# Low halves written over the raw weight tile, four tiles of high halves, and a raw slot that is reloaded after TensorE's use

## The reference, cut to what matters

```python
for l in range(2):
    xn = rmsnorm(x, norm1_g)
    u  = xn @ w_in                                   # 1024 x 9216
    ya, yb, yc, yd = mixers(u)                       # conv, pooling, RG-LRU, conformer conv
    m  = sum_k sigmoid(u_gate_k + b_k) * (y_k @ w_p_k)
    x  = x + m @ w_out
    xn = rmsnorm(x, norm2_g)
    q  = xn @ peer_wq;  s = q . keys                 # top-16 per head, softmax gates
    x  = x + sum over chosen experts of gate * gelu(xn . u_tab[e]) * v_tab[e]
y = rmsnorm(x, final_g)
```

## Time and profile before

| | us |
|---|---|
| three runs: median (lowest to highest) | 2685.22 (2684.17 to 2688.6) |
| profiled execution, its own time | 2685.49 |
| its span, first to last instruction | 2683.4 |
| TensorE matmuls, busy | 2602.2 |
| Pool, busy | 1981.5 |
| DVE, busy | 1512.3 |
| ACT, busy | 1444.6 |

### The profile page before, as it was taken

One profiled execution on the slowest core, in us unless ns is written; L12 is line 12 of the kernel. 1 busy time (PEld: TensorE's weight loads), 2 busy tenths in 40 slices (PEclk: granted clock), 3 DMA queues, 4 the chain that ended last, 5 costly groups with the idle time before them and its releaser, 6 DMA issues. The chain is left out here.

```text
span 2683.4 us, 58960 instructions
## 1 busy us (share of the span) xinstructions
PE 2602.2 (97%) x19532; PEld 2584.3 (96%) x19532; DVE 1512.3 (56%) x3456; ACT 1444.6 (54%) x2996; POOL 1981.5 (74%) x1528
## 2 busy tenths in 40 slices
PE   6999989999999999999989999999999999999997
PEld 6999989999999999999989998899999999999997
DVE  6588232995578733333375863249936786333333
ACT  4764544444666544444447645444456665444444
POOL 6788666888655688888777876668875557888885
PEclk9999999999999999999999999999999999999999
DMA  5555654555433455555454556444553334555554
GB/s 173 152 154 161 157 164 137 169 164 165 133 117 110 135 164 164 181 165 164 150 155 151 159 155 170 158 141 157 169 164 120 113 116 143 163 164 181 165 164 137
DMA packets 126362, 410.67 MB, mean 153 GB/s; under 512 B 20160, under 2 KB 24640, under 8 KB 125504
## 3 DMA queue, kind: packets, MB, share of 16 engines
q1 hardware_dynamic: 120304, 403.37, 48.7%
q10 hardware_dynamic: 5968, 6.22, 1.0%
HBM read 403.32 MB, written 6.22 MB: 153 GB/s over the span
## 5 line engine op out<-in xcount | busy, mean ns | idle before, releaser
L586 POOL TENSOR_TENSOR w_low<-raw,w_high 128x512 fp32r<-128x512 f32 x1498 | 1964.5, 1318 | 660.6 <-ACT w_high L872 463.5
L872 ACT ACTIVATE w_high<-raw 128x512 fp32r<-128x512 f32 x1298 | 817.7, 633 | 1006.2 <-PE bank L623 993.3
L621 PE MATMUL bank<-xn_high,w_high 128*128 128x288 f32 x3456 | 1040.5, 301 | 41.3 <-DVE xn_low L372 27.8
L622 PE MATMUL bank<-xn_low,w_high 128*128 128x288 f32 x3456 | 1023.4, 296 | 0.0
L623 PE MATMUL bank<-xn_high,w_low 128*128 128x288 f32 x3456 | 1020.3, 295 | 0.0
L621 PEld LDWEIGHTS bank<-xn_high,w_high 128*128 128x128 f32 x3456 | 652.8, 189 | 47.5 <-issue 35.8
L623 PEld LDWEIGHTS bank<-xn_high,w_low 128*128 128x128 f32 x3456 | 654.4, 189 | 0.0
L622 PEld LDWEIGHTS bank<-xn_low,w_high 128*128 128x128 f32 x3456 | 654.0, 189 | 0.2
L621 PE MATMUL bank<-c_hi,w_high 128*128 128x288 f32 x2048 | 605.8, 296 | 0.0
L623 PE MATMUL bank<-c_hi,w_low 128*128 128x288 f32 x2048 | 605.8, 296 | 0.0
L622 PE MATMUL bank<-c_lo,w_high 128*128 128x288 f32 x2048 | 605.6, 296 | 0.0
(11 more groups left out here) (237 smaller groups left out, 2419.2 us busy)
## 6 DMA issues: line engine op xcount, KB each, us to landing
raw<-w_u SPq DMA_DIRECT2D x256, 512.0 KB, 3.5
raw<-w_v SPq DMA_DIRECT2D x256, 512.0 KB, 3.5
raw<-w_in_t SPq DMA_DIRECT2D x136, 512.0 KB, 3.5
raw<-w_q SPq DMA_DIRECT2D x32, 512.0 KB, 3.5
raw<-w_ab SPq DMA_DIRECT2D x32, 256.0 KB, 3.1
raw<-w_c SPq DMA_DIRECT2D x16, 512.0 KB, 3.6
raw<-w_out_t SPq DMA_DIRECT2D x16, 512.0 KB, 3.8
raw<-w_first SPq DMA_DIRECT2D x12, 512.0 KB, 3.5
```

Of the source, the lines that this page charges most:

```text
L586: nc.gpsimd.tensor_tensor(w_low[slot][:, :, :], raw[s][:, 4 * half:4 * half + 4, :], w_high[slot][:, :, :].bitcast(F32), ALU.subtract)\
L621: nc.tensor.matmul(out, high, m_high, start=start, stop=False)
L622: nc.tensor.matmul(out, high, m_low, start=False, stop=False)
L872: A(w_high[2 * (s % 2) + half][:, :, :], raw[s][:, 4 * half:4 * half + 4, :], ACT.Copy)\
```

## The change

The four half slots of `w_high` become eight, so each of the four tiles has its own. The eight half slots of `w_low` lie where the raw tiles lie: Pool writes the low half over the half of the raw tile that it reads. The memory used is the same. Slots are now 2 * s + half in `split`, `low`, `halves` and the gated groups; line 1124, in the last V group, is left as it was. ACT's wait before a split (for TensorE, two tiles back) is gone in `split`; in the gated groups it stays. SP waits before a load for `half_done` of the tile four back, that is for TensorE's last use, and likewise before the next layer's first loads. In V's loop ACT waits for the end of tile n before it overwrites `c_high`.

```diff
@@ -179,8 +179,8 @@
         xl = place("xn_low", o_x + KC * T, [KC, T], F32R)
         o_w = o_x + 2 * KC * T
         raw = [place(f"raw{s}", o_w + s * DM, [KC, P]) for s in range(RING)]
-        w_high = [place(f"w_high{s}", o_w + 4 * DM + s * 512, [4, P], F32R) for s in range(RING)]
-        w_low = [place(f"w_low{s}", o_w + 6 * DM + s * 512, [4, P], F32R) for s in range(RING)]
+        w_high = [place(f"w_high{s}", o_w + 4 * DM + s * 512, [4, P], F32R) for s in range(2 * RING)]
+        w_low = [place(f"w_low{s}", o_w + s * 512, [4, P], F32R) for s in range(2 * RING)]
         cursor = [o_w + 8 * DM]
 
         def keep(name, shape, dt=F32):
@@ -501,7 +501,7 @@
                 def _(sp):
                     def load(name, g, s, src):
 
-                        sp.wait_ge(low_done, 2 * number(name, g, s) - 2 * RING + 2)
+                        sp.wait_ge(half_done, 2 * number(name, g, s) - 2 * RING + 2)
                         width = WIDTH[name][s]
                         sp.dma_start(raw[s][:, 0:width, :], src.rearrange("p (k m) -> p k m", k=width))\
                           .then_inc(landed[s], 16)
@@ -566,7 +566,7 @@
                     sp.dma_start(par[:, :], params_in[layer + 1]).then_inc(par_in, 16)
                     for s in range(RING):
 
-                        sp.wait_ge(low_done, 2 * (TOTAL - RING + s) + 2)
+                        sp.wait_ge(half_done, 2 * (TOTAL - RING + s) + 2)
                         load_next(sp, layer + 1, s)
 
                 @block.gpsimd
@@ -582,7 +582,7 @@
                             n = 2 if width == 4 else 1
 
                             pool.wait_ge(high_done, 8 * grp + (2 * s + half + n))
-                            slot = 2 * (s % 2) + half
+                            slot = 2 * s + half
                             nc.gpsimd.tensor_tensor(w_low[slot][:, :, :], raw[s][:, 4 * half:4 * half + 4, :],
                                                     w_high[slot][:, :, :].bitcast(F32), ALU.subtract)\
                               .then_inc(low_done, n)
@@ -868,8 +868,7 @@
 
                         act.wait_ge(landed[s], 16 * grp + 16)
                         for half in range(width // 4):
-                            act.wait_ge(half_done, 8 * grp + (2 * s + half - 3))
-                            A(w_high[2 * (s % 2) + half][:, :, :], raw[s][:, 4 * half:4 * half + 4, :], ACT.Copy)\
+                            A(w_high[2 * s + half][:, :, :], raw[s][:, 4 * half:4 * half + 4, :], ACT.Copy)\
                                 .then_inc(high_done, 2 if width == 4 else 1)
 
                     def ahead(name, g, s, following=(8, 8)):
@@ -1075,7 +1074,7 @@
                         act.wait_ge(landed[s2], 16 * grp + 16)
                         for half in range(2):
                             act.wait_ge(half_done, 2 * number("U", g, s) + half + 1)
-                            A(w_high[2 * (s % 2) + half][:, :, :], raw[s2][:, 4 * half:4 * half + 4, :], ACT.Copy)\
+                            A(w_high[2 * s2 + half][:, :, :], raw[s2][:, 4 * half:4 * half + 4, :], ACT.Copy)\
                                 .then_inc(high_done, 1)
                             if half == 1:
                                 if n >= RING:
@@ -1105,6 +1104,7 @@
                     with act.Fori(0, last_v) as g:
                         for s in range(RING):
                             ahead("V", g, s)
+                            act.wait_ge(half_done, 2 * number("V", g, s) + 2)
                             c_split(RING * g + (s + RING), s)
                     for s in range(RING):
                         grp = group("V", last_v)
```

## The result

The changed kernel takes **2696.78 us** (median of 14 runs, 2692.77 to 2698.49) where the kernel before, on the same chip, takes 2685.77. The ratio is 1.0033, with a 95% interval from 1.0026 to 1.0041. I had forecast 2681.7 us with a range up to 2690.5. The change costs 11 us; I had it gaining 3.5.

The account below looks back on a forecast made before the run. TensorE, busy 97% and gapless in the expert products, was the bound; only idle time between stages could shrink. Terms summed to -1.6 us per layer, -1.7 with branch stalls, -3.5 for two: 2681.7 us, range 2675 to 2690.5.

Parts of the forecast that it names:

- S, -0.4: Section S: with the split done early, ACT's evacuation toward the first recurrent gate begins sooner, -0.4 us per layer.
- the rule: Skill page: two-SBUF-input VectorE instructions and GpSimd instructions reading SBUF shut each other out for a whole instruction.
- (1) ACT may split as soon as it has landed: Everywhere: a tile's second half no longer waits for TensorE, so ACT is freed about 0.54 us earlier per tile.
- (2) The load starts after TensorE's last use: Everywhere: loads start later; a 6.2 us round trip fits 9.7 us of room in the expert products, costing zero.
- XB's 0.3 us to spare: XB and XA branches: room of 6.5 us against a round trip of 6.2, so zero cost, but thin.
- DG, +1.05: DG: the fifth tile's load queues behind four state stores, delaying the split that releases the eighth tile, +1.05 us per layer.
- DP and OUT, -1.1: DP and OUT: four slots cut narrow-tile stalls, -1.9 us to OUT's start, part given back; net -1.1 per layer.
- First pairs, -0.53: After the two tiles that begin a norm (B and WQ): the third tile's second half splits earlier, -0.53 us per layer.
- D, -0.65: Section D: the evacuation before d_val no longer stands behind a 0.54 us split, -0.65 us per layer.
- rivals B: XB and XA: the slot's round trip exceeds the room, 9.6 us more, 2691 us, slower by 0.2%; chance 0.16.
- a remark of 1 us a layer: Back-to-back Pool halves could hold a two-input VectorE instruction 2.5 us; only in XB, up to 1 us a layer: 2683.7.

Follow-up runs that it names:

- e4: The changed kernel with low halves in four slots of their own and loads as early as before the change; 2673.88 us, ratio 0.9952.
- e2: The changed kernel with ACT's wait before each half, for TensorE two tiles back, restored and loads still late; 2697.78 us, ratio 1.0044.
- e5: e4 with one edit: a load starts only when TensorE has used the raw slot; 2697.95 us, ratio 1.0045.
- e1: The changed kernel with Pool waiting in sections B and C until TensorE has used the half two tiles back; 2692.61 us, ratio 1.0025.
- e6: The changed kernel with the five state stores moved from DG to OUT, one after each of ACT's first five steps; 2684.32 us, ratio 0.9986.
- b3: e4 with the five state stores moved from DG to OUT, one after each of ACT's first five steps; 2670.62 us, ratio 0.9943.
- b4: The kernel of b3 measured once more, against the kernel before; 2671.26 us, ratio 0.9943.

## Why the prediction was wrong, point by point

**What failed first: "S, -0.4".** The prediction followed ACT's chain to rg and took what VectorE delivers to S as given. ACT's part of it was fair: in e4, where S begins in time or 0.7 us late, S takes 11.39 and 11.46 us instead of 11.79. What failed is that S's start was held fixed. In the changed kernel S began later: +3.31 and +1.66 ahead of it and +1.07 and +0.93 in it, the latter mostly the lower clock behind the stall. The missing reading was one line of the trace before: first xc_low ends 87.60, S begins 88.62, so 1.0 us of spare for a chain of 30 us that runs beside Pool. The prediction even quoted the rule, and applied it to c_lo and XB alone. There it came out the other way: c_lo, 1196 ns in the earlier trace rows and 1190 over all its 256 executions, has a mean of 504 ns in the changed kernel, 176 us less in all, which is more than the 158 us that VectorE's busy time fell by. In 217 of the 256 Pool stands still when c_lo starts; before, it did in 4. Nothing on TensorE waits for it.

**"(1) ACT may split as soon as it has landed" had a consequence that I priced at nothing.** ACT's wait for TensorE, which looked like pure loss, was what kept Pool's halves apart in the kernel before. In layer 0 of e2 that wait is back, and with it 20 gaps and a chain of 29.86 us; in layer 1 the chain stays at 31.1 us. It isn't the only way: in e4 ACT doesn't wait, the loads are early and Pool waits for TensorE itself, and the chain takes 29.9 and 31.0 us.

**"(2) The load starts after TensorE's last use": the round trip was fair, the list of places too short.** U and V stay without gaps, as said. XB's 0.3 us to spare held roughly: +0.37 and +0.45, one stall of about 0.5 at its end. But the step charged the late loads only where they miss their due time. In e5 against e4 they cost 22.4 us, because every narrow section lives on tiles that are ready long before. I compared the change with the kernel before and never with the same change without late loads, so I didn't see that they took away more than the high slots gave.

**DG, +1.05.** The readings were right, and what was made of them wasn't. ACT reaches the stores 0.25 us earlier, measured from XA's first matmul, where I said 0.3. The fifth tile's load lands after 11.3 us, as taken from the earlier trace rows. But the end of the first stall, for which I had -0.3, comes 1.2 us later in layer 0 and 2.2 in layer 1, since the stores now hold ACT for 7.58 us instead of 6.11 (8.02 instead of 5.72); and the clock falls behind it. The late fifth tile then cost nothing of its own, because everything had slid back by then: the stall at the eighth tile shrank from 1.24 to 0.74 us instead of growing. Of DG's 2.05 and 3.10 us the stalls make 0.7 and 1.7; the rest is about what 3.5 us at a clock of 0.55 cost. Why the stores' issues take longer isn't settled: loads ran beside them before as well.

**DP and OUT, -1.1.** The hold of the last product by the last merge was +0.8 and measured 0.81 us. The gain up to OUT's start was -1.9 and measured -1.03 and -1.02: stalls of 0.4 to 0.6 remained, and one of 1.14 (layer 1: 0.87) in front of OUT. The net is -0.15. e4 shows that four slots can give 2.58 here, if loads come early.

**First pairs, -0.53, and D, -0.65.** The resume gap after WQ's pair is gone and WQ gains 0.30 and 0.38; the gap of 0.27 behind B's pair is gone as well, though nothing of it reaches S. D and A gain 0.30 and -0.08 (e4: 0.5).

**What had no term at all** is the clock. In the changed kernel each stall of 2.3 to 4.1 us ahead of S and in DG was followed by some 3.5 us at a granted clock of 0.50 to 0.55, which I read off for no stretch of the kernel before, although hid such a stretch behind the 1.69 us stall of layer 1. The length of the stall alone doesn't settle it: behind DG's stall of 3.2 us in e2 the clock stayed at 1.00, and behind e1's stall of 2.14 us ahead of S it was 0.55.

Of the rivals B had the right sign and the wrong place. The slower case that came true, a second engine shut out by the rhythm of a third, was in the text as a remark of 1 us a layer.

## What to carry to other kernels

A wait that an engine "loses" may be what spaces the work of the next engine; before it is removed, look at every engine that runs beside that next one, and at how much spare its own deliveries have (here 1.0 us under a chain of 30). When a change bundles a gain and its price, compare it also with the gain alone: early high halves with early loads are worth 12 us here, and the late loads take 24. The stores belong where the tiles have time to spare; whether one per tile is better than five in a row there wasn't tried by itself.

## What the runs showed of the hardware that I had not expected

Two-operand VectorE instructions on 16 columns take 166 to 190 ns alone and 1150 to 1320 ns when one of Pool's halves is already running; three that started within 0.02 us of a half's start took some 163 ns. A chain that needs 11.55 us with Pool's work cut to 4 of 128 columns takes 29.8 to 35.2 us beside all of it. Where Pool's gaps fall seems to decide, not how many there are: within the chain of layer 0, e4 and e5 both have 8 of more than 0.15 us, with 29.85 and 33.03 us. A 512 KB load issued by SP amid five stores issued in a row on ACT's queue lands after 7.3 to 11.8 us in the changed kernel, one issued beside single stores after 5.8 to 7.7 in e6 and 7.3 to 11.0 in b3, and an undisturbed one after 3.5. Behind one and the same stall of 1.69 us the granted clock stayed up in some executions and fell to about 0.6 over the next 4 us in others, worth 1.2 to 1.4 us each time; b3 and b4, one and the same kernel, show both in layer 1 (234.07 and 232.74 us).
